# Two mixture-of-experts stages on one core: expert rows added to x by accumulating indirect transfers, the last two experts by products with 0/1 matrices

## The reference

```python
p_group = softmax(tok @ w_router_group); grp = argmax(p_group)
e_logits = (tok @ w_router_expert)[grp's four experts]
top_p, top_i = top_k(softmax(e_logits), 2)
weight = p_group[grp] * top_p / sum(top_p)
expert = grp * 4 + top_i
y_e = (silu(xb @ w1[e]) * (xb @ w3[e])) @ w2[e]     # 16 experts, 512 hidden features
out[token] += y_e * weight                          # two experts to a token
x = x + gate * out
```

## Time and profile before

| | |
|---|---|
| median of 3 runs | 3422.28 us (3422.06 to 3422.34) |
| the profiled execution, its own time | 3421.25 us |
| its span, first to last instruction | 3419.3 us |
| TensorE busy, mean granted clock | 3224.4 us (94%), 0.968 |
| VectorE, ScalarE, GpSimd busy | 2051.6, 1436.3, 256.5 us |

### The profile page before, as it was taken

One profiled execution on the slowest core, in us unless ns is written; L12 is line 12 of the kernel. 1 busy time (PEld: TensorE's weight loads), 2 busy tenths in 40 slices (PEclk: granted clock), 3 DMA queues, 4 the chain that ended last, 5 costly groups with the idle time before them and its releaser, 6 DMA issues. The chain is left out here.

```text
span 3419.3 us, 40162 instructions
## 1 busy us (share of the span) xinstructions
PE 3224.4 (94%) x15436; PEld 2597.3 (76%) x15436; DVE 2051.6 (60%) x2658; ACT 1436.3 (42%) x1942; POOL 256.5 (8%) x219
## 2 busy tenths in 40 slices
PE   7999998999999999998999989888999789999995
PEld 6888776788878888767888878546688678877884
DVE  5555426555445544355555454554899868868997
ACT  4222225322222222344222232463688547636884
POOL 0000000000000000000000000341122200001331
PEclk9999999999999999999999989899999899999998
DMA  5332221334223331351333241300999621129995
GB/s 203 130 147 110 91 92 34 129 154 159 92 92 148 143 131 57 129 130 74 147 130 129 80 153 40 81 1 25 370 417 415 277 98 59 62 76 382 415 418 232
DMA packets 100134, 534.86 MB, mean 156 GB/s; under 512 B 21952, under 2 KB 22848, under 8 KB 51600
## 3 DMA queue, kind: packets, MB, share of 16 engines
q1 hardware_dynamic: 88752, 491.94, 37.8%
q0 software_dynamic: 6624, 24.12, 1.9%
q10 hardware_dynamic: 4608, 16.78, 1.2%
HBM read 509.64 MB, written 32.07 MB: 158 GB/s over the span
## 5 line engine op out<-in xcount | busy, mean ns | idle before, releaser
L454 ACT ACTIVATE ffn_silu_gate<-ffn_gate_up 128x512 f32<-128x512 f32 x88 | 52.6, 598 | 944.7 <-PE ffn_gate_up L117 944.7
L516 DVE TENSOR_TENSOR ffn_product<-ffn_silu_gate,ffn_gate_up 128x512 f32<-128x512 f32 x88 | 60.5, 688 | 549.1 <-ACT ffn_silu_gate L454 549.1
L2793 DVE TENSOR_TENSOR moe_low<-moe_raw,moe_high 128x2048 fp32r<-128x2048 f32 x144 | 344.6, 2411 | 30.8 <-ACT moe_high L2687 30.7
L115 PE MATMUL ffn_down<-ffn_down_high,ffn_hid_high 128*128 128x512 f32 x704 | 278.9, 396 | 0.5 <-DVE x_tok L540 0.5
L540 DVE SCALAR_TENSOR_TENSOR x_tok<-ffn_down,x_tok 128x512 f32<-128x512 f32 x352 | 232.3, 688 | 77.4 <-PE ffn_down L117 73.8
L2687 ACT ACTIVATE moe_high<-moe_raw 128x2048 fp32r<-128x2048 f32 x144 | 274.2, 1917 | 9.8 <-PE moe_bank L117 9.8
L116 PE MATMUL ffn_down<-ffn_down_low,ffn_hid_high 128*128 128x512 f32 x704 | 277.9, 395 | 0.0
L117 PE MATMUL ffn_down<-ffn_down_high,ffn_hid_low 128*128 128x512 f32 x704 | 277.7, 394 | 0.0
L115 PE MATMUL ffn_gate_up<-ffn_h_high,w 128*128 128x512 f32 x704 | 276.7, 393 | 0.0
L116 PE MATMUL ffn_gate_up<-ffn_h_low,w 128*128 128x512 f32 x704 | 274.6, 390 | 0.0
L117 PE MATMUL ffn_gate_up<-ffn_h_high,w 128*128 128x512 f32 x704 | 274.6, 390 | 0.0
(11 more groups left out here) (613 smaller groups left out, 7356.3 us busy)
## 6 DMA issues: line engine op xcount, KB each, us to landing
moe_raw<-in_moe_w SPq DMA_DIRECT2D x192, 1024.0 KB, 8.3
ffn_raw_gate_up<-in_ffn_gate_up SPq DMA_DIRECT2D x85, 1024.0 KB, 5.8
ffn_ada_w<-in_ada_w SPq DMA_DIRECT2D x32, 1536.0 KB, 7.1
ffn_raw_down<-in_ffn_down SPq DMA_DIRECT2D x88, 512.0 KB, 3.5
mixer_w_raw<-in_mix_w SPq DMA_DIRECT2D x22, 1024.0 KB, 5.1
hgrn_w_raw<-in_hgrn_w SPq DMA_DIRECT2D x19, 1024.0 KB, 5.0
moe_y<-moe_y ACTq DMA_DIRECT2D x32, 512.0 KB, 7.6
nsa_w_raw<-in_nsa_w SPq DMA_DIRECT2D x13, 1024.0 KB, 6.2
```

What stands on the lines that cost most here:

```text
L115: pe.matmul(out, lhsT[0], rhs[0], start=first, stop=False)
L454: act.activation(silu_gate[slot][:, :], gate_up_ps[2 * slot][:, :], ACT.Silu).then_inc(silu_done, 1)
L516: dve.tensor_tensor(product[slot][:, :], silu_gate[slot][:, :], gate_up_ps[2 * slot + 1][:, :], ALU.mult)\
L2793: dve.tensor_tensor(low[n % SPLITS][:, :, :], raw[n % RAWS][:, :, :], high[n % SPLITS][:, :, :].bitcast(FP32), ALU.subtract)\
```

## The change

- **Routing weights fold into the rows.** The lists made with `in_slot` now hold the weights beside the token numbers (`slot_weight`), and `take_y` scales by them. The five operations that make `weight` move ahead of the first expert.
- **Experts 0 to 13** are added to x by eight indirect transfers with an addition (`add_rows`), four for the first choice and then four for the second, each of which waits for the first on its tile. A token whose expert is 14 or 15 reads a row of zeros. They start when y of experts 0 to 13 is stored; the y of 13 is stored by SyncE.
- **Experts 14 and 15** stay in SBUF: VectorE takes y with weight and gate (`take_last`), ScalarE rounds it, VectorE makes the rest (`split_last`), and TensorE multiplies both by 0/1 matrices `pickT` (`pick_rows`, 32 products of 512 columns). VectorE adds the sums to x in eight halves (`add_picked`). The matrices are made by GpSimd (`make_pick`, 8 operations), turned by TensorE (`turn_pick`, 8 transposes) and evacuated by ScalarE (`take_pick`).
- **Order of the last chunks:** g15, u15, d14, d15; the hidden rows of 15 are turned between the two chunks of d14.
- **Numbering of slots** moves from behind the loop into it, at u3, u5, u7 and u9. The count for the overflow branch is loaded at u13 on ScalarE and VectorE.
- **The output** is stored tile by tile inside `moe_1`; the stage `store` is gone. SyncE's overflow branch now comes behind the wait for those stores.

```diff
-    for e in range(NE + 1):
-        for kind, owner in (("g", e), ("d", e - 1), ("u", e)):
+    order = [part for e in range(NE - 1) for part in (("g", e), ("d", e - 1), ("u", e)) if part[1] >= 0]
+    for kind, owner in order + [("g", NE - 1), ("u", NE - 1), ("d", NE - 2), ("d", NE - 1)]:
...
+        def add_rows(pool, t, a, at_slot):
+
+            return pool.indirect_dma_start(chip.x[:, t, :], None, dram["moe_y"],
+                                           bass.IndirectOffsetOnAxis(at_slot[:, a * TT + t:a * TT + t + 1], 0), compute_op=ALU.add)
...
+        sum_bank = [[ps[4], ps[5]], [ps[7], ps[0]], [ps[1], ps[6]], [ps[2], ps[3]]]
+
+        def pick_rows(pe, e, t):
+            for half in range(2):
+                cols = slice(512 * half, 512 * half + 512)
+                pe.wait_ge(last_ready, 2 * (e - NE + BY_PICKS) + half + 1)
+                pe.matmul(sum_bank[t][half][:, :], pickT[:, e - NE + BY_PICKS, t, :], y_high[e % 2][:, cols],
+                          start=(e == NE - BY_PICKS), stop=False)
+                last = pe.matmul(sum_bank[t][half][:, :], pickT[:, e - NE + BY_PICKS, t, :], y_low[e % 2][:, cols],
+                                 start=False, stop=(e == NE - 1))
...
+            e = NE - BY_PICKS - 1
+            sp.wait_ge(y_gated, e + 1)
+            sp.dma_start(dram["moe_y"][P * e:P * e + P, :], y[e % 2][:, :]).then_inc(y_stored[e % 2], 16)
+            if out is not None:
+                for t in range(TT):
+                    sp.wait_ge(x_added, 2 * t + 2)
+                    sp.dma_start(out[0, P * t:P * t + P, :], chip.x[:, t, :]).then_inc(chip.stored, 16)
+                sp.wait_ge(chip.stored, 16 * TT)
             overflow_sync(sp)
...
-                if (kind, e, i) == ("d", NE - 1, 0):
-                    turn_hid(pe, e)
+                if (kind, e, i) == ("d", NE - 2, 1):
+                    turn_hid(pe, NE - 1)
...
+                if (kind, e) == ("d", NE - 1):
+                    pe.wait_ge(last_taken, i + 1)
...
+            pick_rows(pe, NE - 2, 0)
+            pick_rows(pe, NE - 2, 1)
+            pick_rows(pe, NE - 1, 0)
+            pick_rows(pe, NE - 1, 1)
+            pick_rows(pe, NE - 2, 2)
+            pick_rows(pe, NE - 1, 2)
+            pe.wait_ge(last_taken, 2 * BY_PICKS)
+            pick_rows(pe, NE - 2, 3)
+            pick_rows(pe, NE - 1, 3)
...
             for i in range(2):
-                pool.wait_ge(y_stored[i], 16 * (NE // 2))
-            fetch_pairs(pool, fetched)
+                pool.wait_ge(y_stored[i], 16 * (NE // 2 - 1))
+            for t in range(TT):
+                add_rows(pool, t, 0, slot_i).then_inc(rows_added[t], 16)
+            for t in range(TT):
+                pool.wait_ge(rows_added[t], 16)
+                add_rows(pool, t, 1, slot_i).then_inc(rows_added[t], 16)
...
+            def add_picked(t):
+                dve.wait_ge(rows_added[t], 32)
+                for half in range(2):
+                    cols = slice(512 * half, 512 * half + 512)
+                    dve.wait_ge(rows_picked, 2 * t + half + 1)
+                    dve.tensor_tensor(chip.x[:, t, cols], chip.x[:, t, cols], sum_bank[t][half][:, :], ALU.add).then_inc(x_added, 1)
...
+                if (kind, e, i) == ("u", 3, 0):
+                    number_blocks()
+                if (kind, e, i) == ("u", 5, 0):
+                    number_slots()
+                if (kind, e, i) == ("u", 7, 0):
+                    choose_slots()
+                if (kind, e, i) == ("u", 9, 0):
+                    list_blocks()
```

More of the change, by code:

```diff
@@ L2670, in _ @@
                     if kind == "d":
-                        last = split_matmul(pe, ps[2 + i][:, :], (hidT_high[:, k, :], hidT_low[:, k, :]), [w[:, k, :] for w in parts],
+                        hidden = (last_hidT_high, last_hidT_low) if e == NE - 1 else (hidT_high, hidT_low)
+                        last = split_matmul(pe, ps[2 + i][:, :], [what[:, k, :] for what in hidden], [w[:, k, :] for w in parts],
                                      k == 0, k == 3)
@@ L2754, in _ @@
                     make_high(n + 3)
-            store_y(NE - 1)
-            overflow_scalar(act)
-            combine_scalar(act)
+            for i in range(2 * BY_PICKS):
+                e, half = NE - BY_PICKS + i // 2, i % 2
+                act.wait_ge(last_taken, i + 1)
+                act.activation(y_high[e % 2][:, 512 * half:512 * half + 512], y[e % 2][:, 512 * half:512 * half + 512], ACT.Copy)\
+                    .then_inc(last_high, 1)
+            if out is None:
+                for t in range(TT - 1):
+                    act.wait_ge(x_added, 2 * t + 2)
+                    square_tile(act, chip, t, junk[t]).then_inc(tile_squared, 1)
+            overflow_scalar(act, count)
         @block.gpsimd
@@ L2913, in _ @@
                     make_low(n + 2)
-            own(dve.tensor_scalar(over[:, 1, :], count, float(P), None, ALU.is_gt))
-            for i in range(2, 4):
-                own(dve.scalar_tensor_tensor(out=over[:, i, :], in0=count, scalar=float(i * P), in1=over[:, i - 1, :],
-                                             op0=ALU.is_gt, op1=ALU.add))
-            ends = over[:, 4, :]
-            own(dve.tensor_tensor_scan(ends, chip.ones[:, 0:NE], over[:, 3, :], 0.0, ALU.mult, ALU.add))
-            own(dve.tensor_tensor(over[:, 5, :], ends, over[:, 3, :], ALU.subtract))
@@ L2966, in program @@
+            split_last(NE - 1, 0)
+            split_last(NE - 1, 1)
+            for t in range(TT):
+                add_picked(t)
+            overflow_vector(dve, blocks)
 def program(nc, dram, out):
@@ L2980, in program @@
         hgrn(chip)
-        moe(chip, "moe_1", 1)
-        store(chip, out)
+        moe(chip, "moe_1", 1, out=out)
 def constants():
```

311 lines of the change are left out of this document (184 added, 127 removed).

## The result

| | before | after |
|---|---|---|
| median of the runs | 3422.31 us (3422.06 to 3426.31) | 3395.23 us (3391.69 to 3403.51) |
| ratio, 95% interval | | 0.9918 (0.9904 to 0.9933) |
| the profiled execution, its own time | 3421.25 us | 3403.51 us |
| its span; granted clock | 3419.3 us; 0.968 | 3401.7 us; 0.974 |

27.1 us faster at the median, where 39.5 were forecast: the right sign, inside the range of 3377 to 3400, and 12.2 us above the number. The profiled execution of the change happens to be the slowest of its four. The stage of experts has to be read by lengths inside one execution. I cut each profile at four points, two to a stage: the start of the first product on `moe_high` of an expert stage (line 115), and the end of the last addition to x ("x ready").

The account below looks back on a forecast made before the run. TensorE, 94% busy, bounds the kernel, except at both expert stages' ends, where it idles over 20 us. Terms 17.43 + 0.6 + 17.05 + 4.45 = 39.5 us off 3421.25 make 3381.7; the median lies 1.0 above, so 3383, range 3377 to 3400.

Parts of the forecast that it names:

- Order of the last chunks: End of each expert stage: d14 covers making u15's hidden rows, 3.49 us off; new turns add 0.88, a wait 0.25.
- Products with the 0/1 matrices: On TensorE behind d15: 32 products take 7.30 us, with y15's second half ready just in time.
- Adding to x: VectorE, end of both expert stages: most additions lie under the products; x ready 17.05 us earlier in the second, 17.43 in the first.
- I take the plain pace, as the nearest row: The eight transfers with addition: 1.25 us each, as for plain ones, so they are covered; room used up near 2.5.
- The last would land about 2 us later, and the sum would stand: The eight transfers at half rate: 2.5 us each in place of 1.25, using up the room at no cost.
- Store of x: From x ready to the kernel's end: 4.1 us in place of 8.55, 4.45 less, including 0.7 for count load and branch.
- Start of the next stage: Behind the first expert stage: less TensorE idle time raises the clock over 9 us, 0.6 us gained, bounds 0 and 4.1.
- The hidden parts: Transfers, slot numbering and lists, weights' operations, ScalarE's evacuations and GpSimd's eight operations lie under other work and cost nothing.
- the rival of the inserts: In the expert loop: VectorE's 29 inserted operations per stage are not hidden, 13.6 us if all go to TensorE, 3397; chance 0.12.
- Quarter rate: At both stage ends: transfers with addition take 5 us each, a quarter of the plain rate, giving 3409; chance 0.10.
- slower: At both stage ends: GpSimd's transfers, at 7 us each, become the end and cost 5.5 and 9.6 us, 3437; chance 0.04.

Follow-up runs that it names:

- oldorder: The changed kernel with the old order of the last chunks (g15, d14, u15, d15), hidden rows of 15 turned ahead of d15; 3396.28 us, ratio 0.992.
- v2old: v2 with the old order of the last chunks (g15, d14, u15, d15); 3384.64 us, ratio 0.9876.
- plain: The changed kernel with the same sixteen transfers of add_rows but without the addition, so they write over x; 3389.05 us.
- none: The changed kernel without the sixteen add_rows transfers, semaphores raised by GpSimd; expert stages 290.08 and 290.21 us, total 3768.41 us with the overflow code running.
- again: The changed kernel once more, nothing edited, for a second profile; 3394.23 us, ratio 0.991.
- spfix: The changed kernel with y13's store issued ahead of the next stage's first weight load, and the overflow count loaded ahead of the output's stores; 3388.59 us, ratio 0.9894.
- lateout: The changed kernel with all four stores of the output behind the last addition to x; 3399.85 us.
- v2: spfix with the second choices of tiles 0 and 1 by plain transfers, added by VectorE, and transfers issued in a new order; 3384.15 us, ratio 0.9875.
- v2b: v2 once more, on another chip; 3386.58 us, ratio 0.9888.
- before2: The kernel before the change once more, nothing edited, for a second profile; 3434.78 us.

## Why the prediction was right and wrong, step by step

1. **Order of the last chunks: right in the sum, but not all of it is the order's.** TensorE stands 0.30 us ahead of d15, where the forecast allowed 0.25, and d15's last product comes after 281.2 us against a forecast of 280.9. `oldorder` and `v2old` take the order back: 3.7 us where the clock falls after the gap, 2.1 where it does not. They keep the two turns of the 0/1 matrices, so the forecast's figure for them is 3.49 - 0.25 = 3.24. Most of the 1.1 us that are missing had gone with another part of the change. In the kernel before, GpSimd multiplies y of expert 14 beside VectorE's last split ahead of the hidden rows, and both are long:

```profile
3373.71 3.59 POOL L2764 TENSOR_TENSOR moe_y<-moe_y,moe_gate_row 128x1024 f32<-128x1024 f32 x1 [13.45 <-ACT moe_y L2707]
```

```profile
3375.47 3.98 DVE L2793 TENSOR_TENSOR moe_low<-moe_raw,moe_high 128x2048 fp32r<-128x2048 f32 x1 [0.43 <-ACT moe_high L2687]
```

Elsewhere they take 2.41 and 2.28 us. The change has no such multiplication, and in `v2old` the hidden rows are turned 1.23 us after u15's last product against 2.05 before, 0.82 sooner. The rows show the overlap and the lengths; no run takes this multiplication away alone. What I had also not seen is that the order covers for the transfers: alone it is worth 0.3 to 0.5 us.
2. **Products with the 0/1 matrices: right.** 32 in 3392.18 + 0.23 - 3384.87 = 7.5 us, forecast 7.30.
3. **Adding to x: 0.7 us too low** where no transfer is late (290.1 against 289.4, `plain` and `none`): 0.3 of it is step 1's, and 0.24 the products' of step 2.
4. **"I take the plain pace, as the nearest row": this step failed.** The transfers with the addition land 2.5 us apart at best and 2.5 to 2.9 in most steps, not 1.25 (207 GB/s against 387). One step in each end of the change and of `again` is 3.6 to 4.2 us, for a reason that no run shows, so that the mean of an end is 2.7 to 2.9. The plain ones of `plain` land 1.25 us apart where their issues allow it, and 2.1 in the mean. By itself the half rate would have just fitted: the text put the point where room is used up near 2.5, and x is late over `plain` by less than the start was (3.0 against 3.8 us, and 6.1 against 7.4, worked out below). The Trainium skill, "Collectives: The Full Stack", section "The bandwidth ceiling: the fold count and why AG ≠ RS ≠ AR", gives two source reads as the reason for the half rate of the adding step of a ring of cores; the trace agrees with the half rate for the fastest steps, and does not show the reads. "The last would land about 2 us later, and the sum would stand" was wrong because the start was late as well. Forecast was 3364.2, or 9.3 us before u15's last product (3373.46 in the changed order). Measured are 5.5 before in `moe_1` (3367.33 against 3372.80), 3.8 late, since from its issue to GpSimd's release the store of y13 took 7.25 us (3360.08 to 3367.33), where the forecast's start left it 3.4; and 1.9 before in `moe_0`, 7.4 late, where SyncE held the store back 2.5 us more. The text named the queues that a step is moved past in other places, but never asked what stands ahead of the store in SyncE's. Its own range for the last landing also went to 3393.2, 0.7 us past the 3392.5 at which tile 3 was wanted, and it called the transfers covered all the same. Half rate and late start together: 3.0 and 6.1 us over `plain`; `plain` shows that without the half rate the late start costs nothing, and `spfix` that without SyncE's part of the late start in `moe_0` the half rate costs 1.9 to 2.9 there.
5. **Store of x: 5.1 us for 4.1.** 3.0 of landing for 2.6, and 2.04 behind it for 0.73 + 0.7. In all five profiles that have the count's load there (the change, `again`, `plain`, `oldorder`, `lateout`) the part behind the last landing is 2.04 to 2.05 us, in the six that have it moved 1.44 to 1.48, and 0.72 before. So the load is worth 0.6 us, near its term, and another 0.7 was put at nothing; what it is stays open. The landing of the last store varies from 2.7 to 4.9 us, in `v2` and `v2b` alone from 3.5 to 4.9, so that the rest behind x as a whole does not show such a difference. The early stores also cost x 1.3 to 1.4 us (`lateout`), which no step had.
6. **Start of the next stage: 0.6 forecast; -0.7 in the profile of the result, 1.1 to 4.8 in the other eleven with this end** (365.2 before; 365.85, and 360.42 to 364.10). TensorE sat idle 9.59 us ahead of it in `again`, not 5.5 (5.32 in `v2`), and a stretch far behind was not in my bounds at all. The 9 us in which the next stage starts, in the change:

```profile
2741.90:2750.90 9.00, 8.43 (x31) 6.81 (x31) 7.76 (x14) 5.72 (x9) 0.00 (x0) 0.50 0.62 255
```

The same in `again`:

```profile
2738.43:2747.43 9.00, 8.31 (x38) 6.22 (x38) 7.76 (x14) 6.58 (x11) 0.00 (x0) 0.75 0.62 254
```

In the kernel before the granted clock was 0.50 there, as in the earlier trace rows. From x ready to the start of `moe_1`'s routing (ScalarE's `moe_h_tok<-x_tok`) the kernel before takes 326.3 us. The six profiles with this end whose clock was 0.50 to 0.53 in the 9 us take 326.2 to 326.9, no gain; the six at 0.73 or more take 325.1 to 325.5, 0.8 to 1.2 less. So the 0.6 stood in the middle of two outcomes. The larger part lies behind it, in the routing, down to `moe_1`'s first product. The kernel before, the change, and `again`:

```profile
3065.38:3104.25 38.87, 36.35 (x175) 22.68 (x175) 29.06 (x76) 16.37 (x21) 2.24 (x1) 0.87 0.85 321
```

```profile
3064.47:3103.45 38.98, 36.15 (x175) 22.08 (x176) 31.75 (x84) 16.49 (x21) 3.70 (x2) 0.87 0.86 330
```

```profile
3059.61:3095.18 35.57, 33.32 (x175) 20.85 (x175) 30.17 (x83) 16.60 (x21) 2.33 (x1) 0.95 0.90 350
```

The same 175 products take 3.4 us less at a granted clock of 0.95 in the mean than at 0.87. The short routing is not the change's doing as such: in `moe_0` the kernel before has it as well, 35.5 us in its first profile, and 38.9 in `before2`, and the change has 38.8 and 38.9 there. In `moe_1` both profiles of the kernel before have the long one, and two of the twelve with the new end. Why the clock falls in some executions and not in others is open, and so is whether the change makes the long one rarer in `moe_1`.

The hidden parts stayed hidden: the time of an expert is 17.72 us, also at u3, u5 and u7; only at u9 it is 17.82, and 18.21 where a 0/1 matrix is turned. So the rival of the inserts is out, but for 0.1 us to a stage. Quarter rate and slower are out by the mean of 2.9. GpSimd's four operations of 128x128 take 13.41 us together, one 0.79 and one 7.00, and lie under its idle time as I had it.

## What to carry to other kernels

When a wait is replaced by transfers that are to be hidden, work out when the last one lands from its real start: follow the store that it waits for through its own queue, with all that stands ahead of it, and take an addition in the transfer at twice the plain time until a trace says otherwise. Where two changes each uncover an end, neither shows its worth alone: the order of the chunks was worth 0.5 us with the transfers late, and 2 to 3.5 with them on time. And where single executions differ by more than the effect, cut the profile into stages and compare these.

## What the runs showed of the hardware that I had not expected

- Indirect transfers of 512 KB that add into SBUF: one in 2.5 us at best and in 2.7 to 2.9 in the mean of eight, DMA engines fully busy at 195 to 207 GB/s; the issue takes GpSimd 1.54 us at least, against 0.93 for the same transfer without the addition (`plain`).
- GpSimd's `tensor_scalar` of 128x128 f32 with two scalars per partition: 3.3 us in the mean of the 16, but 0.79 to 7.00 for a single one; its addition of 128x1024: 2.38 to 2.83.
- A VectorE subtraction that meets a GpSimd addition: 2.67 us instead of 0.69. A VectorE split beside a GpSimd multiplication, in the kernel before: 3.98 us instead of 2.28.
- The granted clock after a gap of TensorE of some 3 us ahead of d15: 1.00 in the four ends of the kernel before and in one of `v2old`, about half for 3 us in the three other ends with the old order. The routing of an expert stage, the same 175 products: 35.6 us at 0.95 in the mean, 38.9 at 0.87. The first product of `moe_0` starts from 2427 to 2445 us in executions of code that differs only in the routing just ahead of it.
